# Gated heads in pairs with token-major values, and three orders outside the heads

## The chip, the cores and the metric

The kernel runs on one core of one Trainium2 chip. The metric is the time of one execution in device microseconds. Five engines work side by side from queues of their own: TensorE (PE) multiplies, VectorE (DVE) and ScalarE (ACT) work on elements and read and write TensorE's accumulators (PSUM), GpSimd (POOL) makes masks and issues transfers, SyncE (SP) issues the loads of the weights. They wait for one another by counting semaphores: `wait_ge(S[name], n)` holds the engine's queue until the counter has reached n.

## What is computed

Two transformer blocks over 512 tokens of 1024 channels, batch 1, one layer each, all in float32. What matters for the change is the mixing part of the first block and the start of attention in the second:

```python
# first block: 8 heads, each with a gated linear-attention branch (a) and a stick-breaking branch (b)
h = rms_norm(x, g); p = h @ w_in          # q_a k_a (64 wide) v_a o_a (128), i f, q_b k_b v_b (128), g_a g_b (128)
qk_a = silu(causal_conv([q_a, k_a], conv_w))
h_a  = head_rms_norm(mlstm(q_a, k_a, v_a, i, f)) # decay-masked scores times v_a, over a denominator
y_a  = sigmoid(o_a) * h_a
z    = rms(q_b) . rms(k_b) / sqrt(128)           # strictly causal
A    = sigmoid(z) * prod_{s<j<t} (1 - sigmoid(z_tj))
y_b  = A @ v_b
y    = sigmoid(g_a) * y_a + sigmoid(g_b) * y_b
x    = x + y @ w_out;  x = x + relu(rms_norm(x) @ w_up)**2 @ w_down
# second block: latent attention (8 heads), and sparse attention (8 heads), which sees the 128 best keys of an index
score = sum_h relu(q_idx_h . k_idx) * w_h        # 8 index heads
sel   = top_k(score, 128)                        # found in 16 rounds of 8
```

## The kernel before

**Projections.** All weights lie in one array `wall` of groups, 1024 x 512 each. SP loads a group in two halves into `w_raw`; ACT rounds a half to `w_hi` (`split_hi`, L257) and DVE makes the rest `w_lo` (`split_lo`, L264). `project` (L271) makes one tile, 128 x 512 results, by 24 matmuls: 8 row blocks times (hi x hi, hi x lo, lo x hi). Its first row block waits for the first half of the group's `w_lo`, its fifth for the second half. Tiles alternate between two PSUM banks `proj[:, 0]` and `proj[:, 1]`: tile n waits (`tile_free`) until tile n - 2 is evacuated, and `tile_made` counts finished tiles. `w_hi`/`w_lo` have two slots; a group's split waits until the group two before it has had its last tile.

**The heads of the first block.** A loop over eight heads on each engine; the order is written out by hand. Per head there are two groups and eight tiles, all feature-major (weight stationary, activation moving): 0 q_b, 1 k_b, 2 q_a with k_a, 3 v_b, 4 v_a, 5 o_a, 6 g_a, 7 g_b. PE's order (`head`, L1395) is: tiles 0, 1, 2; sums of squares of q_b and k_b into `pa` (L1424, L1425); tile 3; stick scores z into `pa` (L1430); tiles 4, 5; the turns of `v_bT` and `v_aT` to token-major in `pa` (L1439, eight transposes by matmul with the identity); gated scores into `pm` (L1446); tile 6; turns of the stick weights `beta` (L1456); weighted sums with `v_a` (L1462); tile 7; turns of `y_tok` (L1468); the weighted sum with `v_b` (L1411). The tiles between steps give ACT, DVE and POOL time for what the next step reads.

**What ACT does in a head.** It copies tiles out of `proj`, gives the roots (Ln, Exp), the Sigmoids of z (`beta`, `keep`) and of the convolution (`silu`), the Exp of `decay` (L581), copies of the turned values and sticks (L583 to L588), the row variances (L592). Gates o and g_a are first copied (L579, L586) and made Sigmoids in place later (L600, L601); g_b is a Sigmoid straight from `proj` (L603). Sigmoid and Exp lie in different tables, so there are table loads.

**What DVE and POOL do in a head.** DVE: `sq_lo`, norms of q_b and k_b, four taps of the convolution, `decay` arguments, silu, four scans (`kept`) and the product `beta`, then `split_lo`, then `decay` times scores (L1000); POOL masks its diagonal blocks (L449) before PE's weighted sums. `y_tok` (L1015) follows the variances; then the gated sums and y_hi, y_lo. `head_done` is counted at the end; the next head's squares wait for it.

**The start.** x comes in four tiles; each is scaled by DVE and turned by PE (`norm_pe`, L336); ACT and DVE make `h_hi` and `h_lo` (L319, L329); then come the gate tile (L1380), whose rows ACT and DVE work on, and the first head's tiles. Tile 2 waits for ACT's copy of tile 0, which stands behind the gate rows on ACT.

**The second block.** For each of four token blocks, `latents(t)` makes four tiles with few row blocks, which `latent_evac` (L681, copies at L689) takes out of `proj`. `idx_pair(p)` makes index scores of two heads in `pa` and `pm`; ACT's `idx_rel` (L701) takes them out as relus, 1280 columns each. Pair p waits for `2 * p` relus. On ACT, after the relus of pair 0, `latent_evac(2)` follows, and after those of pair 1, `latent_evac(3)`. In attention, B = 0 to 3 are pairs of latent heads and B = 4 to 7 pairs of sparse heads. DVE takes row maxima (L1250), divides (L1261), and in each B below 4 runs four rounds `top(B, rnd)` (L1267, L1271), each of which finds the next eight of each query's best keys. After 16 rounds the mask `idx` is made, which B = 4 needs.

Of the kernel before, what the change touches and what calls it, by code (L numbers as in the profile page):

```python
# [13 lines left out]
P = 128  # L14
# [8 lines left out]
DQK_A = 64  # L23
HD_B = 128
# [17 lines left out]
TRI_COLS = 1280  # L42

# [34 lines left out]
def program(nc, x_in, wall, gains, head_par, sb_gains, b_if, *rest):  # L78
    *block2_in, out = rest
    with ExitStack() as ctx:  # L80
# [41 lines left out]
        def at(name, offset, shape, dt=F32):  # L122
# [13 lines left out]
        names = "q_b k_b sq_q sq_k conv silu k_a v_bT v_aT v_b gate_o gate_a gate_b".split()  # L136
        (q_b, k_b, sq_q, sq_k, conv, silu, k_a, v_bT, v_aT, v_b, gate_o, gate_a, gate_b) = [
            at(n, (61 + 2 * i) * K, [P, SEQ]) for i, n in enumerate(names)]
        v_a = at("v_a", 87 * K, [P, TB, P + 1])
        y_tok, scl = sq_k, silu  # L140
# [272 lines left out]
        def _(pool):  # L413
# [11 lines left out]
            gp.memset(v_a[:, :, P:P + 1], 1.0).then_inc(S["consts"], 1)  # L425
# [73 lines left out]
        def _(act):  # L499
# [39 lines left out]
            with a.Fori(0, HEADS) as h:  # L539
                n = T_HEADS + 8 * h  # L540
                ga = G_HEADS + 2 * h

                a.preload_act_table_set("natural_log_exp_and_others")
                split_hi(ga + 1, 0, 0)

                for j, (raw, sq) in enumerate(((q_b, sq_q), (k_b, sq_k))):
                    a.wait_ge(S["tile_made"], n + j + 1)
                    a.wait_ge(S["head_done"], h + 1)
                    a.activation(raw[:, :], proj[:, j], ACT.Copy)
                    a.activation(sq_hi[:, j], proj[:, j], ACT.Square)  # L550
                    a.activation(sq[:, :], proj[:, j], ACT.Square).then_inc(S["tile_free"], 1)
                split_hi(ga + 1, 0, 1)

                a.wait_ge(S["tile_made"], n + 3)
# [9 lines left out]
                a.wait_ge(S["tile_made"], n + 4)  # L564
                a.activation(v_bT[:, :], proj[:, 1], ACT.Copy).then_inc(S["tile_free"], 1)
                split_hi(ga + 2, 1, 0)
# [5 lines left out]
                a.wait_ge(S["tile_made"], n + 5)  # L572
                a.activation(v_aT[:, :], proj[:, 0], ACT.Copy).then_inc(S["tile_free"], 1)

                a.activation(silu[:, :], conv[:, :], ACT.Sigmoid).then_inc(S["silu_sig"], 1)
                a.preload_act_table_set("natural_log_exp_and_others")
                split_hi(ga + 2, 1, 1)
                a.wait_ge(S["tile_made"], n + 6)
                a.activation(gate_o[:, :], proj[:, 1], ACT.Copy).then_inc(S["tile_free"], 1)  # L579
                a.wait_ge(S["arg_a"], 4 * h + 4)  # L580
                a.activation(decay[:, :], decay[:, :], ACT.Exp).then_inc(S["decay_exp"], 1)  # L581
                a.wait_ge(S["v_turned"], h + 1)
                a.activation(v_b[:, :], pa[:, 0:512], ACT.Copy).then_inc(S["v_sb"], 1)  # L583
                a.activation(v_a[:, :, 0:P], pa[:, 512:1024].rearrange("p (t n) -> p t n", t=TB), ACT.Copy).then_inc(S["v_sb"], 1)
                a.wait_ge(S["tile_made"], n + 7)
                a.activation(gate_a[:, :], proj[:, 0], ACT.Copy).then_inc(S["tile_free"], 1)  # L586
                a.wait_ge(S["a_turned_b"], h + 1)
                a.activation(aT[:, :], pa[:, 0:TRI_COLS], ACT.Copy).then_inc(S["a_b"], 1)  # L588

                a.wait_ge(S["num_made"], h + 1)  # L590
# [8 lines left out]
                a.wait_ge(S["tile_free"], n + 7)  # L599
                a.activation(gate_o[:, :], gate_o[:, :], ACT.Sigmoid).then_inc(S["gate_sig"], 1)  # L600
                a.activation(gate_a[:, :], gate_a[:, :], ACT.Sigmoid, bias=par[:, 5:6]).then_inc(S["gate_sig"], 1)  # L601
                a.wait_ge(S["tile_made"], n + 8)
                a.activation(gate_b[:, :], proj[:, 1], ACT.Sigmoid, bias=par[:, 6:7]).then_inc(S["tile_free"], 1)  # L603
# [134 lines left out]
            idx_rel(0)  # L738
            idx_rel(1)
            latent_root(1)  # L740
            for t in (2, 3):
                latent_evac(t)
                if t == 2:
                    evac(N_Q[1], q_b2[:, 1])
                latent_squares(t)
                idx_rel(2 * t - 2)
                idx_rel(2 * t - 1)
                latent_root(t)
# [152 lines left out]
        def _(dve):  # L901
# [4 lines left out]
            v.memset(tick[:, 2:3], 0.0).then_inc(S["pad_zero"], 1)  # L906
            def square_sum(t):
# [42 lines left out]
            with v.Fori(0, HEADS) as h:  # L950
                ga = G_HEADS + 2 * h

                v.wait_ge(S["head_done"], h + 1)
# [4 lines left out]
                split_lo(ga + 1, 0, 0)  # L958
                for j, sq in enumerate((sq_q, sq_k)):
                    v.wait_ge(S["tile_free"], T_HEADS + 8 * h + j + 1)  # L960
                    v.tensor_tensor(sq_lo[:, j], sq[:, :], sq_hi[:, j], ALU.subtract).then_inc(S["sq_lo"], 1)
                split_lo(ga + 1, 0, 1)
# [310 lines left out]
            for B in range(4):  # L1273
# [13 lines left out]
                for rnd in range(4):  # L1287
                    top(B, rnd)
# [83 lines left out]
        def _(pe):  # L1372
# [22 lines left out]
            def head(h, first=False):  # L1395
# [21 lines left out]
                if first:  # L1417
                    gate_rows()
# [55 lines left out]
            with t_.Fori(1, HEADS) as h:  # L1474
                head(h)
# [307 lines left out]
```

## Time and profile before

| | us |
|---|---|
| median of 3 runs | 1264.02 (1262.86 to 1264.53) |
| profiled execution, its own time | 1262.79 |
| its span, first to last instruction | 1260.5 |
| PE busy | 1240.2 (98%) |
| DVE busy | 694.1 (55%) |
| ACT busy | 606.6 (48%) |
| POOL busy | 47.8 (4%) |

The span is what the profile's times count in; the execution has 2.3 us around it. Busy PE includes modelled ends of matmuls, so a short wait between two of them can hide in it.

### The profile page before, as it was taken

The page shows a single profiled execution, that of the slowest core. Times are in us where ns is not written, and L with a number is a line of the kernel's source. Part 1 is how long each engine was busy: PE and PEld are TensorE (multiplying, and loading weights), DVE is VectorE, ACT ScalarE, POOL GpSimd, SP SyncE. Part 2 cuts the span into 40 slices and gives each one's busy share as a digit, 9 for nine tenths or more (in the row PEclk, how much of TensorE's full clock was granted, in tenths as well). Part 3 has the DMA queues.
Part 4 walks back from the last instruction along what each step waited for, and adds up shares of the span by engine and source line. Part 5 has one row for each costly group of instructions (what it writes and reads, how often), then busy time and mean ns, then how long its engine had stood idle before and what let it go on. Part 6 is the DMA issues. An engine that isn't in the chain of part 4 may idle for free.

```text
span 1260.5 us, 15952 instructions
## 1 busy us (share of the span) xinstructions
PE 1240.2 (98%) x5912; PEld 1008.2 (80%) x5912; DVE 694.1 (55%) x1179; ACT 606.6 (48%) x894; POOL 47.8 (4%) x146
## 2 busy tenths in 40 slices
PE   6999999999999999999999999999999999999998
PEld 5788888888888888888888888888867777677787
DVE  6646455554645555552443433445468989666671
ACT  6745565564556563441321421335456655566820
POOL 1000000000000020000000000000000000000000
PEclk9999999999999999999999999999999999999999
DMA  6323222132322234223231322333213233535621
GB/s 219 110 75 100 75 67 87 64 100 75 100 75 67 85 125 168 68 88 113 68 132 67 100 100 100 101 108 150 76 67 110 104 119 129 201 126 166 251 67 67
DMA packets 26398, 134.48 MB, mean 107 GB/s; under 512 B 3224, under 2 KB 4312, under 8 KB 13552
## 3 DMA queue, kind: packets, MB, share of 16 engines
q1 hardware_dynamic: 16992, 107.49, 25.3%
q0 software_dynamic: 4752, 16.92, 3.9%
q10 hardware_dynamic: 4608, 9.44, 2.0%
q8 instruction: 32, 0.52, 0.2%
q14 instruction: 14, 0.11, 0.0%
HBM read 122.28 MB, written 11.55 MB: 106 GB/s over the span
## 4 chain that ended last, share of the span: by engine, by line
PE 84%; DVE 10%; ACT 3%; issue 2%; DMA 1%; ACTq 0%; DVEq 0%; SPq 0%
PE proj L294 74%; DVE idx L1271 2%; DVE w_lo L267 2%; DVE top L1267 2%; PE pm L1462 1%; PE pa L1411 1%; PE pa L1430 1%; DVE p_sb L1250 1%; PE pm L1446 1%; PE pa L1648 1%; ACT w_hi L261 1%; PE pa L1456 1%; ACT p_sb L792 1%; DVE p_sb L1261 1%; DVE idx L1164 1%
## 5 line engine op out<-in xcount | busy, mean ns | idle before, releaser
L294 PE MATMUL proj<-h_hi,w_hi 128*128 128x512 f32 (+1 forms) x976 | 385.7, 395 | 2.0 <-DVE w_lo L267 1.0
L294 PE MATMUL proj<-h_hi,w_lo 128*128 128x512 f32 (+1 forms) x976 | 377.1, 386 | 0.0
L294 PE MATMUL proj<-h_lo,w_hi 128*128 128x512 f32 (+1 forms) x976 | 376.7, 386 | 0.0
L267 DVE TENSOR_TENSOR w_lo<-w_raw,w_hi 128x2048 fp32r<-128x2048 f32 x100 | 227.9, 2290 | 89.8 <-ACT w_hi L261 88.9
L261 ACT ACTIVATE w_hi<-w_raw 128x2048 fp32r<-128x2048 f32 x100 | 189.8, 1912 | 127.0 <-PE proj L294 121.3
L294 PEld LDWEIGHTS proj<-h_hi,w_hi 128*128 128x128 f32 x976 | 183.4, 188 | 46.0 <-issue 9.9
L294 PEld LDWEIGHTS proj<-h_lo,w_hi 128*128 128x128 f32 x976 | 183.5, 188 | 38.3 <-issue 2.9
L294 PEld LDWEIGHTS proj<-h_hi,w_lo 128*128 128x128 f32 x976 | 183.3, 188 | 37.5
L294 PE MATMUL proj<-w_hi,act_hi 128*128 128x512 f32 x256 | 99.8, 390 | 0.0
L294 PE MATMUL proj<-w_lo,act_hi 128*128 128x512 f32 x256 | 99.6, 389 | 0.0
L294 PE MATMUL proj<-w_hi,act_lo 128*128 128x512 f32 x256 | 99.6, 389 | 0.0
L1097 DVE TENSOR_TENSOR x_res<-x_res,proj 128x512 f32<-128x512 f32 x32 | 21.9, 686 | 92.2 <-PE proj L294 92.2
L633 ACT ACTIVATE relu<-proj 128x512 f32<-128x512 f32 x32 | 19.2, 599 | 106.5 <-PE proj L294 106.5
L1083 DVE TENSOR_TENSOR relu_sq<-relu 128x512 f32<-128x512 f32 x32 | 22.2, 694 | 73.4 <-ACT relu L633 73.4
L294 PE MATMUL proj<-w_hi,h_hi 128*128 128x512 f32 (+1 forms) x160 | 62.2, 389 | 0.0
L294 PE MATMUL proj<-w_lo,h_hi 128*128 128x512 f32 (+1 forms) x160 | 61.9, 387 | 0.0
L294 PE MATMUL proj<-w_hi,h_lo 128*128 128x512 f32 (+1 forms) x160 | 61.7, 386 | 0.0
L294 PEld LDWEIGHTS proj<-w_hi,act_lo 128*128 128x128 f32 x256 | 48.1, 188 | 10.0
L294 PEld LDWEIGHTS proj<-w_lo,act_hi 128*128 128x128 f32 x256 | 48.1, 188 | 10.0
L294 PEld LDWEIGHTS proj<-w_hi,act_hi 128*128 128x128 f32 x256 | 48.1, 188 | 9.8
L792 ACT ACTIVATE p_sb<-p_sb,mx 128x128 f32<-128x128 f32 (+1 forms) x64 | 35.1, 550 | 31.8 <-DVE mx L1253 31.8
L294 PEld LDWEIGHTS proj<-w_hi,h_hi 128*128 128x128 f32 x160 | 30.0, 188 | 7.4 <-issue 1.5
(394 smaller groups left out, 1650.2 us busy)
## 6 DMA issues: line engine op xcount, KB each, us to landing
w_raw<-in_wall SPq DMA_DIRECT2D x100, 1024.0 KB, 5.1
gates<-gate_st ACTq DMA_DIRECT2D x24, 256.0 KB, 2.1
m_all<-gates POOLq DMA_DIRECT2D x2, 1280.0 KB, 7.5
x_res<-in_x ACTq DMA_DIRECT2D x4, 512.0 KB, 5.2
bc<-gate_rows POOLq DMA_DIRECT2D x8, 256.0 KB, 3.5
x_res<-in_x POOLq DMA_DIRECT2D x4, 512.0 KB, 4.8
x<-x_res POOLq DMA_DIRECT2D x1, 2048.0 KB, 7.4
g_all<-gates POOLq DMA_DIRECT2D x1, 2048.0 KB, 11.2
```

The source lines that it names most:

```text
L261: nc.scalar.activation(w_hi[:, slot, 4 * half:4 * half + 4, :], w_raw[:, half], ACT.Copy)\
L267: nc.vector.tensor_tensor(w_lo[:, slot, 4 * half:4 * half + 4, :], w_raw[:, half], w_hi[:, slot, 4 * half:4 * half + 4, :], ALU.subtract)\
L294: mm = nc.tensor.matmul(proj[:, bank, 0:cols] if tokens else proj[:, bank, toks], lhsT, rhs, start=(k == 0 and q == 0), stop=(k == kts - 1 ...
L633: a.activation(relu[:, i % 2], proj[:, i % 2], ACT.Relu).then_inc(S["tile_free"], 1)
L792: a.activation(x, x, ACT.Exp, bias=mx[:, u, i:i + 1], accum_out=row_sum[:, u, i:i + 1])\
L1083: v.tensor_tensor(relu_sq[:, i % 2], relu[:, i % 2], relu[:, i % 2], ALU.mult).then_inc(S["a_sq"], 1)
L1097: v.tensor_tensor(xx, xx, proj[:, t % 2], ALU.add).then_inc(S["tile_free"], 1)
L1164: v.scalar_tensor_tensor(idx[:, c], rel[h % 2][:, c], w_idx[:, i, h:h + 1], idx[:, c] if h else causal[:, 384 - P * i:512], ALU.mult, ALU. ...
L1250: v.tensor_tensor_reduce(p_sb[u][:, c], X[:, c], mask(i), scale(i), -3.0e38, ALU.add, ALU.max, mx[:, u, i:i + 1]).then_inc(S[f"smax{u}"], 1)
L1261: v.tensor_scalar(x, x, row_sum[:, u, i:i + 1], None, ALU.mult).then_inc(S[f"p_norm{u}"], 1)
L1267: v.max(top8[:, i - 1, :], idx[:, LOW[i]:LOW[i] + P * (i + 1)]).then_inc(S["top_max"], 1)
L1271: v.match_replace(x, top8[:, i - 1, :], x, TAKEN).then_inc(S["top_out"], 1)
```

## The change

- **Pairs.** The heads run as four pairs, three in a loop and the last written out (`more=False`). A pair has four groups and sixteen tiles, numbered from 0: 0 q_b, 1 k_b, 2 q_a with k_a, 3 o_a (head one); 4 to 7 values; 8 g_a, 9 g_b (head one); 10 q_b, 11 k_b, 12 q_a with k_a, 13 o_a, 14 g_a, 15 g_b (head two). A pair's first two tiles are made inside the pair before (16 and 17, counted from its start); those of the first pair ahead of the loop.
- **Token-major values.** Tiles 4 to 7 are one token block each: activation stationary, weight moving, with v_b of both heads and v_a of both heads as 512 columns. ACT copies them straight to `v_b` and `v_a`. The turns of values, `v_bT` and `v_aT` are gone.
- **Gates.** o and g_a are made Sigmoids straight from `proj`; the copies are gone.
- **PE's order in a pair.** Head one: tile 2; squares; 3; z; 4, 5; gated scores; 6, 7; turns of beta; weighted sums; 8; turns of y; weighted sum with v_b. Head two: 9, 10, 11, 12; squares; 13; z; 14, 15; gated scores; 16; turns of beta; weighted sums; 17; turns of y; weighted sum with v_b. In the last pair 16 and 17 are left out.
- **pv_read.** The squares of a head wait for DVE's read of the last v_b sum, not for the whole head's end. `y_tok` has room of its own.
- **Outside the heads.** PE turns the identity 36 times before x is there (`WARM`). ACT's `latent_evac(2)` stands between `idx_rel(0)` and `idx_rel(1)`, `latent_evac(3)` between `idx_rel(2)` and `idx_rel(3)`. The first of the 16 rounds runs before B = 0; each of B = 0 to 2 has four rounds and B = 3 has three.

The core of the diff (the bodies of DVE's and ACT's steps, which only moved into functions, are left out):

```diff
+PAIRS = HEADS // 2
+QKA, O_A, VALUES, G_A, G_B, NEXT = (2, 12), (3, 13), 4, (8, 14), (9, 15), 16
+WARM = 36
@@ ACT
-            with a.Fori(0, HEADS) as h:
...
+            def qk_tile(n, heads, j):
+                raw, sq = ((q_b, sq_q), (k_b, sq_k))[j]
+                a.wait_ge(S["tile_made"], n + 1)
+                if heads is not None:
+                    a.wait_ge(S["z_made"], heads)
...
+            def gate_tile(n, dst, bias=0.0):
+                a.wait_ge(S["tile_made"], n + 1)
+                a.activation(dst[:, :], proj[:, 0 if dst is gate_a else 1], ACT.Sigmoid, bias=bias).then_inc(S["tile_free"], 1)
...
+            def value_tile(n, t):
+                a.wait_ge(S["tile_made"], n + VALUES + t + 1)
+                a.activation(v_b[:, :, t], proj[:, t % 2, 0:2 * P].rearrange("p (u d) -> p u d", u=2), ACT.Copy)
+                a.activation(v_a[:, :, t, 0:P], proj[:, t % 2, 2 * P:4 * P].rearrange("p (u d) -> p u d", u=2), ACT.Copy)\
+                    .then_inc(S["tile_free"], 1)
...
+                conv_tile(h, n + QKA[0])
+                gate_tile(n + O_A[0], gate_o)
+                split_hi(g + 2, 1, 0)
+                sticks(h)
+                value_tile(n, 0)
+                a.preload_act_table_set("natural_log_exp_and_others")
+                split_hi(g + 2, 1, 1)
+                value_tile(n, 1)
+                decays(h)
+                value_tile(n, 2)
+                value_tile(n, 3)
+                stick_turns(h)
+                variance(h)
+                split_hi(g + 3, 0, 0)
+                gate_tile(n + G_A[0], gate_a, par[:, 5:6])
+                split_hi(g + 3, 0, 1)
+                gate_tile(n + G_B[0], gate_b, par[:, 6:7])
+                h = 2 * p + 1
+                a.preload_act_table_set("natural_log_exp_and_others")
+                for j in range(2):
+                    qk_tile(n + 10 + j, 2 * p + 1, j)
+                conv_tile(h, n + QKA[1])
+                gate_tile(n + O_A[1], gate_o)
+                split_hi(g + 4, 1, 0)
+                sticks(h)
+                split_hi(g + 4, 1, 1)
+                a.wait_ge(S["par_head"], 3 * h + 3)
+                gate_tile(n + G_A[1], gate_a, par[:, 5:6])
+                gate_tile(n + G_B[1], gate_b, par[:, 6:7])
+                a.preload_act_table_set("natural_log_exp_and_others")
+                decays(h)
+                if more:
+                    split_hi(g + 5, 0, 0)
+                    qk_tile(n + NEXT, 2 * p + 2, 0)
+                stick_turns(h)
+                variance(h)
+                if more:
+                    qk_tile(n + NEXT + 1, 2 * p + 2, 1)
+                    split_hi(g + 5, 0, 1)
@@ ACT, second block
             idx_rel(0)
+            latent_evac(2)
             idx_rel(1)
             latent_root(1)
-            for t in (2, 3):
...
+            evac(N_Q[1], q_b2[:, 1])
+            latent_squares(2)
+            idx_rel(2)
+            latent_evac(3)
+            idx_rel(3)
+            latent_root(2)
@@ DVE (head two of a pair; head one has the same steps)
+                head_start(h)
+                for j in range(2):
+                    square_low(n + 10 + j, j)
+                qk_norms(h)
+                conv_taps(h, n + QKA[1])
+                split_lo(g + 4, 1, 0)
+                decay_args(h)
+                gated_keys(h)
+                sticks(h)
+                split_lo(g + 4, 1, 1)
+                gated_scores(h)
+                if more:
+                    split_lo(g + 5, 0, 0)
+                    v.wait_ge(S["a_done"], h + 1)
+                    square_low(n + NEXT, 0)
+                token_norm(h)
+                gated_y(h, n + O_A[1], n + G_A[1])
+                if more:
+                    square_low(n + NEXT + 1, 1)
+                head_end(h, n + G_B[1])
+                if more:
+                    split_lo(g + 5, 0, 1)
@@ DVE, attention
+            top(0, 0)
             for B in range(4):
...
-                for rnd in range(4):
-                    top(B, rnd)
+                for rnd in range(4 * B + 1, min(4 * B + 5, 16)):
+                    top(rnd // 4, rnd % 4)
@@ PE
+            for i in range(WARM):
+                t_.transpose(pm[:, 1024 + P * (i % 4):1024 + P * (i % 4 + 1)], ident[:, :], ident[:, :])
...
+            def pair(p, more=True):
+                n_v = T_HEADS + 16 * p + VALUES
+                for u in range(2):
+                    h = 2 * p + u
+                    if u:
+                        for j in (9, 10, 11):
+                            head_tile(p, j)
+                    head_tile(p, QKA[u])
+                    square_sums(h)
+                    head_tile(p, O_A[u])
+                    stick_scores(h)
+                    head_tile(p, G_A[1] if u else VALUES)
+                    head_tile(p, G_B[1] if u else VALUES + 1)
+                    gated_scores(h)
+                    if u == 0:
+                        head_tile(p, VALUES + 2)
+                        head_tile(p, VALUES + 3)
+                    elif more:
+                        head_tile(p, NEXT)
+                    stick_turns(h)
+                    gated_sums(h, u, n_v)
+                    if u == 0:
+                        head_tile(p, G_A[0])
+                    elif more:
+                        head_tile(p, NEXT + 1)
+                    head_turns(h, u)
```

## Rows read from the trace of the kernel before

**Rows 1.** The page: busy time of the engines, and the granted clock in 40 slices.

```profile
PE 1240.2 (98%) x5912; PEld 1008.2 (80%) x5912; DVE 694.1 (55%) x1179; ACT 606.6 (48%) x894; POOL 47.8 (4%) x146
...
PEclk9999999999999999999999999999999999999999
```

**Rows 2.** The waits of PE: us in total, times, longest us.

```profile
PE proj L336 <- DVE xs L324: 8.1, 1, 8.1
```

**Rows 3.** Timeline of PE at the start: start, us, line, operands, idle before.

```profile
8.51 0.84 PE L336 MATMUL pa<-ident,xs 128*128 128x128 f32 x3
...
13.73 0.49 PE L336 MATMUL pm<-ident,xs 128*128 128x128 f32 x3
...
35.35 0.50 PE L294 MATMUL proj<-h_hi,w_hi 128*128 128x512 f32 x1 [0.96 <-ACT sq_q L551]
```

**Rows 4.** Timeline of DVE at the start.

```profile
14.35 1.41 DVE L329 SCALAR_TENSOR_TENSOR h_lo<-proj,gain,h_hi 128x512 fp32r<-128x512 f32 x2 [0.69 <-ACT h_hi L319]
```

**Rows 5.** Timeline of PE in the last head.

```profile
446.96 0.60 PE L1439 MATMUL pa<-ident,v_bT 128*128 128x128 f32 x4
...
447.92 0.69 PE L1446 MATMUL pm<-silu,k_a 64*128 64x512 f32 x1
...
449.41 0.50 PE L294 MATMUL proj<-h_hi,w_hi 128*128 128x512 f32 x1
...
455.01 1.25 PE L1456 MATMUL pa<-ident,beta 128*128 128x128 f32 x10
456.10 2.40 PE L1462 MATMUL pm<-v_a,decay 128*128 128x129 f32 x20
458.25 0.48 PE L294 MATMUL proj<-h_hi,w_hi 128*128 128x512 f32 x1
```

**Rows 6.** Timeline of ACT in the last head.

```profile
447.65 1.26 ACT L581 ACTIVATE decay<-decay 128x1280 f32<-128x1280 f32 x1
...
464.01 0.69 ACT L603 ACTIVATE gate_b<-proj,par 128x512 f32<-128x512 f32 x1 [0.51 <-PE proj L294]
464.71 1.28 ACT L604 ACT_TABLE_LOAD   x1
```

**Rows 7.** Timeline of DVE and POOL in the last head.

```profile
448.98 2.28 DVE L267 TENSOR_TENSOR w_lo<-w_raw,w_hi 128x2048 fp32r<-128x2048 f32 x1
451.18 1.49 DVE L1000 SCALAR_TENSOR_TENSOR decay<-pm,decay 128x1280 f32<-128x1280 f32 x1
...
460.97 0.69 DVE L1015 TENSOR_TENSOR sq_k<-pm,tok 128x512 f32<-128x512 f32 x1 [0.51 <-ACT tok L597]
...
452.74 1.03 POOL L449 TENSOR_SCALAR_AFFINE_SELECT decay<-decay 128x128 f32<-128x128 f32 x4 [10.44 <-DVE decay L1000]
```

**Rows 8.** Timeline of PE, then of ACT, at the latent tiles.

```profile
930.25 0.50 PE L294 MATMUL proj<-w_hi,ckv_hi 128*128 128x512 f32 x1 [1.08 <-ACT q_a L689]
...
943.38 0.51 PE L294 MATMUL proj<-w_hi,ckv_hi 128*128 128x512 f32 x1 [1.08 <-ACT q_a L689]
...
944.98 0.37 PE L1547 MATMUL pa<-t_c 32*128 32x128 f32 x1
...
941.18 1.23 ACT L701 ACTIVATE rel<-pm 128x1280 f32<-128x1280 f32 x1
...
945.09 0.60 ACT L689 ACTIVATE v_a<-proj 128x512 f32<-128x512 f32 x1
```

**Rows 9.** Timeline of DVE, then of PE, around the rounds.

```profile
970.55 0.35 DVE L1250 CUSTOM_DVE_ANT_0 p_sb<-pm,causal,qk_ss 128x128 f32<-128x128 f32 x1 [2.72 <-issue]
...
1073.85 0.42 DVE L1267 MAX8 top<-idx 128x8 f32<-128x256 f32 x1
...
1077.07 0.23 DVE L1291 COPY idx<-causal 128x128 f32<-128x128 f32 x1
...
1087.46 1.31 PE L1639 MATMUL pm<-ident,p_sb 128*128 128x128 f32 x10 [1.81 <-DVE p_sb L1261]
1088.86 1.31 PE L1639 MATMUL pa<-ident,p_sb 128*128 128x128 f32 x10
```

More of the change, by code:

```diff
@@ L135, in program @@
         bc = at("bc", 57 * K, [P, SEQ])
[L136 to L140, printed above, removed]
+        q_b, k_b, sq_q, sq_k, conv, silu, k_a = [
+            at(n, (61 + 2 * i) * K, [P, SEQ]) for i, n in enumerate("q_b k_b sq_q sq_k conv silu k_a".split())]
+        v_b = at("v_b", 75 * K, [P, 2, TB, P])
+        gate_o, gate_a, gate_b = [at(n, (79 + 2 * i) * K, [P, SEQ]) for i, n in enumerate(("gate_o", "gate_a", "gate_b"))]
+        v_a = at("v_a", 85 * K, [P, 2, TB, P + 1])
+        y_tok, scl = at("y_tok", 59 * K, [P, SEQ]), silu
         qk_pad = at("qk_pad", 47 * K, [P, 3 + SEQ])
@@ L604, in _ @@
+            with a.Fori(0, PAIRS - 1) as p:
+                pair(p)
+            pair(PAIRS - 1, more=False)
             a.preload_act_table_set("natural_log_exp_and_others")
@@ L1470, in head, with pair @@
                 t_.wait_ge(S["a_b"], h + 1)
[L1471 to L1475 removed]
+                for i in range(TB):
+                    mm = t_.matmul(pa[:, P * i:SEQ], v_b[:, u, i], aT[:, TRI[i]:TRI[i] + SEQ - P * i],
+                                   start=(i == 0), stop=(i == TB - 1))
+                mm.then_inc(S["pv_b_made"], 1)
+            def pair(p, more=True):
+                n_v = T_HEADS + 16 * p + VALUES
[10 more added lines that the diff above has]
+                    head_tile(p, G_B[1] if u else VALUES + 1)
+                    gated_scores(h)
+                    if u == 0:
[10 more added lines that the diff above has]
+                    head_turns(h, u)
+            head_tile(0, 0, first=True)
+            head_tile(0, 1)
+            gate_rows()
+            with t_.Fori(0, PAIRS - 1) as p:
+                pair(p)
+            pair(PAIRS - 1, more=False)
             t_.wait_ge(S["head_done"], HEADS)
@@ L1708, in lay_out, with wide, narrow @@
     wall[G_GATES, :, :, 32:32 + HEADS] = f_a
-    for h in range(HEADS):
-        wide, narrow = slice(P * h, P * (h + 1)), slice(DQK_A * h, DQK_A * (h + 1))
-        wall[G_HEADS + 2 * h] = np.concatenate(
-            [q_b[:, :, wide], k_b[:, :, wide], q_a[:, :, narrow], k_a[:, :, narrow], v_b[:, :, wide]], axis=2)
-        wall[G_HEADS + 2 * h + 1] = np.concatenate([w[:, :, wide] for w in (v_a, o_a, g_a, g_b)], axis=2)
+    def wide(w, h):
+        return w[:, :, P * h:P * (h + 1)]
+    def narrow(w, h):
+        return w[:, :, DQK_A * h:DQK_A * (h + 1)]
+    for p in range(PAIRS):
+        h, i = 2 * p, 2 * p + 1
+        for k, columns in enumerate((
+                (wide(q_b, h), wide(k_b, h), narrow(q_a, h), narrow(k_a, h), wide(o_a, h)),
+                (wide(v_b, h), wide(v_b, i), wide(v_a, h), wide(v_a, i)),
+                (wide(g_a, h), wide(g_b, h), wide(q_b, i), wide(k_b, i)),
+                (narrow(q_a, i), narrow(k_a, i), wide(o_a, i), wide(g_a, i), wide(g_b, i)))):
+            wall[G_HEADS + 4 * p + k] = np.concatenate(columns, axis=2)
     for j in range(2):
```

180 lines of the change are left out of this document (84 added, 96 removed).

## Prediction

> **What bounds the kernel now.** I read the page's busy line first. PE is busy for 98% of the span [rows 1], so a microsecond counts only where PE loses work or where PE waits. DVE at 55% and ACT at 48% matter where PE waits for them. Next I read the waits of PE: its largest entry is the 8.1 us before the first turn [rows 2]. Then I followed the timeline through four places: the start [rows 3, 4], one head [rows 5 to 7], the latent tiles [rows 8] and the sparse half of attention [rows 9]. Matmul ends are modelled there, so I go by starts: 24 matmuls of a tile and the step to the next work take 5.60 us (449.41 to 455.01), 0.23 each. A head is a string of such tiles with PE never waiting. It holds eight tiles before and eight after, so order alone wins nothing there; only PE work that goes, and waits that come, count.
>
> **Part 1, the start: -0.7 us.** The turns of x run at half pace first: three from first start to last end take 0.84 us at 8.51 and 0.49 us at 13.73 [rows 3]. The 36 added turns of the identity (0.21 us each at the low pace, 7.5 us; fewer when the pace has risen) about fill the 8.1 us of [rows 2]. An overrun of a microsecond harms nothing: the x turns behind them, at the full pace, would still catch up with DVE, which scales x tile by tile. They end earlier, about with the last scaled tile. But the end of this stage is not PE's. DVE waits 0.69 us for the first h_hi, until 14.35 [rows 4]; only this can go, for DVE has other work before it and works without a break behind it. The chain runs on through the gate rows to ACT's evacuation, for which PE waits at 35.35 [rows 3]: that start moves to 34.7. Bounds: 1.2 earlier (if the first projection tile, not the gate rows, sets the rest), and 2.5 later if the pace falls back in the pause that the earlier turns leave ahead of the gate matmuls. I take -0.7, because the wait of DVE is a row.
>
> **Part 2a, the heads' work: -7.2 us.** The eight turns of v_bT and v_aT go. PE starts them at 446.96 and the scores behind them at 447.92 [rows 5]: 0.96 us per head, 7.7 for eight. No row shows a projection tile followed at once by the 64-row scores. The step may cost nothing new or up to 0.1 more (8 x 0.1 = 0.8); I take 7.2, a little over half of this off; bounds 6.9 and 7.7. Values are made token by token instead (activation stationary, weight moving). These matmuls are as many and as wide, and cost the same: nothing. ACT loses two gate copies per head and gains none. DVE's work is the same and POOL's and SP's too.
>
> **Part 2b, the pairs' new order: 0 in the first seven heads.** The tightest places, counted in the last head's frame: the scores now end at 448.45 (0.96 before 449.41). In an odd head the next q tile follows at once and asks for the second w_lo half at its fourth row block, 12 x 0.23 later, 451.2. DVE ended that half at 451.26 before [rows 7], but the Sigmoid of conv no longer stands behind the v_aT copy on ACT, which brings DVE's chain about 1.5 us forward: not late. In an even head the sums follow the turns of beta (1.09) and ask for the last value tile's copies, two of 256 columns; ACT is free for them, and I find 0.1 us to spare: nothing, at most 0.3 x 4. The new wait of head_end on the tile of g_b leaves three tiles before pa is wanted again.
>
> **Part 2c, the last head: +7.1 us.** Here no tile is left between the scores and the turns of beta, nor between the sums and the turns of y; before, tiles 6 and 7 stood there. So two waits come into the open:
> - The sums wait for the masked decay. The tile of g_b ends at 446.96 and its Sigmoid starts 0.2 later: 447.2. Behind it on ACT: Sigmoid 0.69, table load 1.28, exponential 1.26 [rows 6], to 450.4. Then DVE's product, whose mask starts 1.56 after it (451.18 to 452.74), and the mask 1.03 [rows 7]: 453.0. PE is through with the turns of beta at 448.45 + 1.09 = 449.55 [rows 5] and waits 3.6 us (start 453.15).
> - The turns of y wait for y_tok. Sums start at 456.10 [rows 5], y_tok ends at 461.66 [rows 7]: 5.56 later. PE's sums take 2.15 of this (456.10 to 458.25). The wait is 5.56 - 2.15 + 0.1 = 3.5 us.
> Together 7.1. Bounds: 5.5 (table load hidden and the y chain a little shorter) and 8.5 (one weight split of 1.9 more ahead of the exponential). In the run of heads the change is thus worth -7.2 + 7.1, about nothing: what the turns give back, the empty last head takes.
>
> **Part 3, the latent tiles: -0.35 us.** PE waits at 930.25 and 943.38 for the copy of q_a, 1.08 each [rows 8], because two relus of 1.23 stand ahead of it. With one relu ahead, the copy starts when its tile is ready: the first wait goes whole, -1.1. The second goes too (943.38 becomes 942.3), but what is late next? The index scores at 944.98 need the fourth relu, now behind the four copies. The v_a copy started at 945.09; 1.1 earlier is 944.0, half a microsecond on ACT, then a relu of 1.24 ends at 945.7: 0.75 later than 944.98. The two together: -1.1 + 0.75. Bounds -1.1 and +1.5.
>
> **Part 4, the first round of the top values: -2.2 us.** At 1087.46 PE waits 1.81 by the view, 1.97 by starts (a modelled matmul end lies 0.16 behind the next start), and 0.25 more before the second batch (1.40 from 1087.46 to 1088.86, where ten turns take 1.09). DVE is late: its last round ran from 1073.85 to 1077.07, 3.2 us [rows 9]. One round now stands ahead of the first latent head, where DVE sat idle for 2.72 before 970.55 and a little more before the weight split ahead of that: 3.2 us about fit. The wait needs 2.2 and gets 3.2. Bounds -2.3 and -1.0 (if the early round delays the maxima).
>
> **Sum**, against the profiled execution's own 1262.8 us: -0.7 - 7.2 + 7.1 - 0.35 - 2.2 = -3.35, hence 1259.4. The median of the runs lies 1.2 above that execution, so I forecast 1264.0 - 3.4 = 1260.6.
>
> **A rule that speaks against it.** In this trace the granted clock never falls in any slice [rows 1], through waits of up to 2.2 us from start to start; the longest behind the start is the one before 1087.46 [rows 9]. The last head will have 3.6 and 3.5 us of wait, with 2.15 of work between. The Trainium skill ("TensorE: Matmul & The Clock Gate", section "HAM oscillation") says that a long enough idle stretch between bursts of matmuls throws the array back to its lower clock, so that the next burst starts slow. By the trace's longest wait alone the sum stays; by that page the second rival below happens. No row here decides it.
>
> **The rivals.**
> - *Shorter waits in the last head* (4.5 instead of 7.1): the chains pass through small ACT and DVE steps that may start earlier. 1258.0. For it: 1.28 of the first chain is a table load, which ACT may take while it waits for the tile. Against it: that load needs the table of exponentials, and the Sigmoid ahead needs the other.
> - *The clock falls in the last head.* After 8.1 idle us the low pace lasted about 5.1 us of work (from 8.1 to about 13.2) [rows 2, 3]. Half pace over 5.1 us costs 2.5; if the sums between the waits run slowly too, 2.1 more. Together 2.5 to 4.7 on the forecast: 1263.1 to 1265.3, I say 1264.0, no change.
> - *Slower: the splits come late at the next q tile.* ACT now has a table load and a Sigmoid of o_a ahead of the split and of beta (1.28 + 0.63, where one copy of 0.6 stood). If DVE's chain of scans, product and split comes x us later than I reckon, the q tile waits x - 1.5 in each of three odd heads, and the last head x - 0.8. From x = 2.2 this eats the 3.4 us, and at x = 3 it gives 4.5 + 2.2 - 3.4 = +3.3: 1267.3. For it: w_lo ended within 0.1 us of that point before. Against: the silu wait that goes is longer than the load that comes.
> - *The first round moves the wait, not the work*: if the maxima of the first latent head slip by what DVE gains later, part 4 gives 0: 1262.8.
>
> **How the numbers follow.** Forecast 0.50 (own range 1258.6 to 1262.4), shorter waits 0.14, clock falls 0.17, slower 0.11, moved wait 0.08. A measurement of this kernel can tell about 0.2% (2.5 us) from no change: faster means below 1261.5, slower above 1266.5. Faster: 0.40 of the forecast, 0.13 of the shorter waits and 0.02 of the others, 0.55. Slower: 0.08 of the slower case and 0.01 of the clock, 0.09. Same: 0.36. For 8 in 10 the range is 1256.5 to 1265.5.
>
> **What would show it.** Right: no row of v_bT or v_aT; each head 0.9 us shorter than before; no PE wait over 0.5 us in the first seven heads; in the last, about 3.6 before the sums and 3.5 before the turns of y; the index scores of the third pair waiting about 1.9; no wait before the turns of p_sb in the first sparse head; granted clock 1.00 from the start on. Wrong: waits at the q tile in the middle of odd heads; ten turns taking 2.1 us behind the last head's waits; a pause over 0.5 us before the sums in even heads.

## The result, and the profile after

The changed kernel is slower: 1268.26 us median (1265.66 to 1270.32, 14 runs) where the kernel before has 1264.49 (1262.5 to 1267.4, 14 runs) on the same chip, ratio 1.0027, 95% interval 1.0019 to 1.0035. The forecast was 1260.6, with 1256.5 to 1265.5 as its range. The profiled execution after took 1269.27, its span is 1267.3.

The page after, busy time of the engines and the granted clock in 40 slices, answers to [rows 1]:

```profile
PE 1246.1 (98%) x5884; PEld 1011.0 (80%) x5884; DVE 694.4 (55%) x1180; ACT 580.3 (46%) x871; POOL 71.1 (6%) x146
...
PEclk9899999999999989999999999999999999999999
```

PE has 28 instructions fewer (36 more turns of the identity, 64 fewer of the values) and is busy for 5.9 us more. Less work that takes longer is slower work, and two slices of PEclk stand at 8. The same in stretches, PE alone (us, busy time and count, granted clock, DMA share, GB/s):

```profile
13.00:20.00 7.00, 4.32 (x13) 0.76 0.65 240
...
36.00:44.00 8.00, 7.24 (x19) 0.57 0.60 179
44.00:460.00 416.00, 415.24 (x1935) 1.00 0.25 81
460.00:475.00 15.00, 9.22 (x36) 0.77 0.35 127
...
940.00:954.00 14.00, 12.15 (x68) 1.00 0.00 1
954.00:962.00 8.00, 8.00 (x30) 0.79 0.00 0
```

Behind the first 6 us the granted clock is 1.00 but for five stretches, in which it is 0.5 (1.2 of 2.4 GHz): from 15.7 (3.4 us), 36.1 (6.8), 462.8, 469.6 and 954.3 (3.4 each). I call such a drop a fall of the clock. In the profile before it is 1.00 at all of these places. Each stretch begins within 0.7 us of the end of a wait, just before it or just behind, but for the last, 1.8 behind one. The waits of PE after (us in total, times, longest):

```profile
PE pm L1560 <- POOL decay L453: 3.3, 1, 3.3
PE pm L1567 <- DVE y_tok L1077: 3.2, 1, 3.2
PE proj L1501 <- DVE h_lo L333: 2.7, 1, 2.7
PE proj L298 <- ACT sq_q L551: 2.3, 1, 2.3
PE pa L1679 <- ACT rel L751: 1.8, 1, 1.8
```

They are the two of the last head, the one before the gate matmuls, the one before tile 2, and the one before the indexer's fifth tile. PE's timeline at four of them:

```profile
12.56 0.49 PE L340 MATMUL pm<-ident,xs 128*128 128x128 f32 x3
15.73 0.76 PE L1501 MATMUL proj<-h_hi,wg_hi 128*128 128x512 f32 x1 [2.68 <-DVE h_lo L333]
...
36.76 0.79 PE L298 MATMUL proj<-h_hi,w_hi 128*128 128x512 f32 x1 [2.29 <-ACT sq_q L551]
...
457.92 1.31 PE L1551 MATMUL pa<-ident,beta 128*128 128x128 f32 x10
462.56 4.14 PE L1560 MATMUL pm<-v_a,decay 128*128 128x129 f32 x20 [3.33 <-POOL decay L453]
469.92 1.12 PE L1567 MATMUL pm<-ident,y_tok 128*128 128x128 f32 x4 [3.21 <-DVE y_tok L1077]
470.83 3.43 PE L1571 MATMUL pa<-aT,v_b 128*128 128x512 f32 x8
...
474.01 0.47 PE L298 MATMUL proj<-w_hi,y_hi 128*128 128x512 f32 x1
```

The twenty sums took 2.40 before [rows 5] and take 4.14 now. A matmul of 512 columns that starts every 0.23 us at the full clock starts every 0.43 inside these stretches.

The stages by starts of PE, for before, after, and the experiment with filler in four of the five waits (e8, below). The boundaries after are these rows (the square sums of heads 0, 2 and 6, the first scores of the sparse half and its first output tile; the first output tile of the gated half is the last row above):

```profile
45.22 0.39 PE L1525 MATMUL pa<-sq_hi,ones_r 128*128 128x512 f32 x1
...
154.04 0.39 PE L1525 MATMUL pa<-sq_hi,ones_r 128*128 128x512 f32 x1
...
371.71 0.39 PE L1525 MATMUL pa<-sq_hi,ones_r 128*128 128x512 f32 x1
...
977.27 0.60 PE L1732 MATMUL pm<-kT,qT 96*128 96x128 f32 x3
...
1176.29 0.50 PE L298 MATMUL proj<-og_hi,w_hi 128*128 128x512 f32 x1
```

| Stage | before, us | after | forecast | with filler |
|---|---|---|---|---|
| to the first square sums | 40.92 | +4.30 | -0.7 | +0.64 |
| six heads | 331.38 | -4.89 | -5.4 | -4.90 |
| last two heads | 94.02 | +8.28 | +5.3 | +5.14 |
| to the sparse scores | 501.86 | +1.40 | -0.35 | -0.24 |
| to the sparse output | 201.33 | -2.31 | -2.2 | -2.31 |
| the rest | 91.03 | +0.01 | 0 | -0.02 |
| span | 1260.54 | +6.79 | -3.35 | -1.69 |

Six of the eight heads, the sparse half and the rest went as forecast. The three stages that hold the five slow stretches went wrong by 5.0, 3.0 and 1.75 us. With filler the same three are shorter by 3.66, 3.14 and 1.64; in the first of them 0.65 is no clock, for there the gate matmuls start at 15.08 instead of 15.73, with weights that came earlier.

### The profile page after: what moved, and what is told of

The parts are those of the page before. It is cut to its first block, busy times and chain, and to the rows that moved or that the text cites. A ratio compares the mean times of both kernels' runs of the same rounds, so it can differ in the third digit from the quotient of the medians.

```text
span 1267.3 us, 15778 instructions
## 1 busy us (share of the span) xinstructions
PE 1246.1 (98%) x5884; PEld 1011.0 (80%) x5884; DVE 694.4 (55%) x1180; ACT 580.3 (46%) x871; POOL 71.1 (6%) x146
## 4 chain that ended last, share of the span: by engine, by line
PE 92%; DVE 5%; ACT 1%; issue 1%; DMA 1%; POOL 0%; ACTq 0%; SPq 0%; DVEq 0%
PE proj L298 79%; PE pm L1560 2%; PE pa L1571 1%; PE pa L1532 1%; PE pa L1780 1%; DVE w_lo L271 1%; PE pm L1542 1%; PE pa L1679 1%; PE pa L1760 1%; DVE idx L1389 1%; PE pa L1771 1%; PE pa L1551 1%; PE proj L1501 1%; DVE p_sb L1368 1%; PE pm L1771 1%
## 5 line engine op out<-in xcount | busy, mean ns | idle before, releaser
L298 PE MATMUL proj<-h_hi,w_hi 128*128 128x512 f32 (+1 forms) x848 | 334.6, 395 | 2.3 <-ACT sq_q L551 2.3
L298 PE MATMUL proj<-h_hi,w_lo 128*128 128x512 f32 (+1 forms) x848 | 328.0, 387 | 0.0
L298 PE MATMUL proj<-h_lo,w_hi 128*128 128x512 f32 (+1 forms) x848 | 327.9, 387 | 0.0
L298 PEld LDWEIGHTS proj<-h_hi,w_hi 128*128 128x128 f32 x848 | 160.1, 189 | 39.0 <-issue 7.3
L298 PE MATMUL proj<-w_hi,h_hi 128*128 128x512 f32 (+1 forms) x288 | 114.6, 398 | 0.0
L298 PE MATMUL proj<-w_hi,h_lo 128*128 128x512 f32 (+1 forms) x288 | 112.1, 389 | 0.0
L298 PE MATMUL proj<-w_lo,h_hi 128*128 128x512 f32 (+1 forms) x288 | 112.1, 389 | 0.0
L298 PEld LDWEIGHTS proj<-w_hi,h_hi 128*128 128x128 f32 x288 | 54.4, 189 | 15.1 <-issue 4.3
L298 PEld LDWEIGHTS proj<-w_hi,h_lo 128*128 128x128 f32 x288 | 54.4, 189 | 11.5 <-issue 1.0
L298 PEld LDWEIGHTS proj<-w_lo,h_hi 128*128 128x128 f32 x288 | 54.4, 189 | 10.7
```

The source lines that it names most:

```text
L298: mm = nc.tensor.matmul(proj[:, bank, 0:cols] if tokens else proj[:, bank, toks], lhsT, rhs, start=(k == 0 and q == 0), stop=(k == kts - 1 ...
```

## The experiments

Theory: the change makes five waits of PE longer or new; behind them the granted clock falls, and the work there runs at half pace. Rivals: the waits themselves cost more than reckoned, or one part alone is to blame. All runs were timed in five rounds against the kernel before on the same chip. Where a difference is said to be by the ratio, it is the ratio's distance from 1, of 1264 us.

**One part undone, or filler in one place.** e1_no_warm takes the early turns out, e2_latent3 moves one copy back, e3_fill gives PE 30 turns of the identity that nothing reads in each of the last head's two waits.

```diff
 e1_no_warm
-WARM = 36
+WARM = 0
 e2_latent3
             idx_rel(2)
-            latent_evac(3)
             idx_rel(3)
             latent_root(2)
+            latent_evac(3)
 e3_fill (the same lines once more behind gated_sums)
                     stick_turns(h)
+                    if u and not more:
+                        fill(p, 30)
                     gated_sums(h, u, n_v)
```

> The changed kernel without the 36 turns of the identity ahead of x (WARM = 0), all else kept. Theory (the clock): the turns let the x turns end 1.3 us earlier, the pause before the gate matmuls grows from 1.7 to 2.8 us, the clock falls in it, the gate rows come 1.4 us late and the clock falls again in the longer wait behind them; by the profile the start costs 4.3 us. Without the turns PE starts tile 2 at about 35.4 again, the clock stays at 1.00 from 13 us on, and the kernel takes 4 us less than the changed one: about 1264.3. Rival (the turns help by the 0.7 us I forecast, and the clock falls there whatever precedes): 1269, and low clock at 16 and at 36 us remains.

> The changed kernel with latent_evac(3) put back behind idx_rel(3) on ACT; latent_evac(2) stays between the first two relus. Theory (the clock): the wait of 2.0 us before the third pair of index scores goes and with it the fall of the clock at 954 us, which costs about 2 us in the profile; the wait of 1.24 us before the third tile of that block comes back. Together 2.8 us less than the changed kernel, about 1265.5. Rival (the new order only trades one wait for another): 0.75 us less, about 1267.5.

> The changed kernel with 30 turns of the identity into an idle accumulator bank in each of the two waits of the last head (before the weighted sums and before the turns of y), 3.3 us each: no wait gets shorter and no work goes. Theory (the clock): the two falls at 462.8 and 469.6 us go, and sums, turns and the v_b sum run at full pace: 3.3 us less than the changed kernel, about 1265.0. Rival (the waits themselves are the cost): within 0.5 us of the changed kernel, 1268.3.

Measured: e1_no_warm 1266.11 (11 runs), ratio 1.0017 (1.0008 to 1.0026); e2_latent3 1265.51 (11), 1.0015 (1.0006 to 1.0024); e3_fill 1265.88 (11), 1.0014 (1.0004 to 1.0023); before 1263.8 (27). They were expected at 1264.3, 1265.5 and 1265.0. By the ratio each gives back 1.3 to 1.6 us of the changed kernel's 3.4, about what the two intervals together leave open (1.5); what is clear is that each is still slower than before, so undoing one part alone does not give the whole back. In e1_no_warm the fall at the gate matmuls is gone, but those before tile 2 (at 35.9) and in the last head are there. In e3_fill the last head keeps its clock, and the indexer's wait still loses it (PE's columns as above):

```profile
455.00:470.00 15.00, 14.94 (x103) 1.00 0.48 175
944.00:952.00 8.00, 7.70 (x25) 0.57 0.00 0
```

**Filler in four of the five places.** e8_fill_all is e3_fill with 20 more turns ahead of tile 2 and 16 ahead of the indexer's fifth tile; the wait before the gate matmuls has none.

```diff
+            for i in range(20):
+                t_.transpose(pa[:, P * (i % 4):P * (i % 4 + 1)], ident[:, :], ident[:, :])
             with t_.Fori(0, PAIRS - 1) as p:
...
             latents(3)
+            for i in range(16):
+                t_.transpose(pa[:, 1408:1536], ident[:, :], ident[:, :])
             idx_pair(2)
```

> The kernel after with turns of the identity that nothing reads in TensorE's waits: 30 in each of the two of the last head, 20 ahead of tile 2, 16 ahead of the second pair of the indexer's tiles. No wait is removed and no real work changed. Theory (the loss against the forecast is the clock): the granted clock stays full in all but the pause before the gate matmuls, and the time goes to 1261.5, below before's 1263.8, though the kernel only got more to do. Rival (the loss is in the waits themselves or in work that grew): the time stays at 1265 or above, as with the filler in the last head alone (1265.9).

Measured: 1260.89 us (1259.92 to 1263.59, 9 runs), ratio 0.9972 (0.9960 to 0.9984); before 1264.33 (26). A kernel that does strictly more than the changed one is 0.55% faster than it. PE's timeline in its last head and at the indexer:

```profile
454.26 1.31 PE L1551 MATMUL pa<-ident,beta 128*128 128x128 f32 x10
455.41 3.44 PE L1578 MATMUL proj<-ident 128*128 128x128 f32 x30
458.91 2.50 PE L1560 MATMUL pm<-v_a,decay 128*128 128x129 f32 x20
461.25 3.44 PE L1578 MATMUL proj<-ident 128*128 128x128 f32 x30
464.63 0.66 PE L1567 MATMUL pm<-ident,y_tok 128*128 128x128 f32 x4
465.12 2.32 PE L1571 MATMUL pa<-aT,v_b 128*128 128x512 f32 x8
467.20 0.47 PE L298 MATMUL proj<-w_hi,y_hi 128*128 128x512 f32 x1
...
943.67 1.91 PE L1721 MATMUL pa<-ident 128*128 128x128 f32 x16
945.65 0.37 PE L1690 MATMUL pa<-t_c 32*128 32x128 f32 x1
```

The sums take 2.50 instead of 4.14; from the turns of beta to the first output tile it is 12.94 us instead of 16.09. The real work waits as long as before; only the array isn't idle. The one fall left lies at the gate matmuls, the one wait without filler (from 14.7 us, 3.4 us). This is the last column of the table: within 1.7 us of the forecast, 1.3 of them in the first stage.

**Each part alone, on the kernel before.** e5_before_warm adds the 36 turns only, e6_before_round the first round only, e10_latents_only the latents' order only, e9_heads_only the pairs only (both orders and the early turns taken out of the kernel after). e11_heads_fill is e9 with e3's filler.

```diff
 e5_before_warm
+            for i in range(36):
+                t_.transpose(pm[:, 1024 + P * (i % 4):1024 + P * (i % 4 + 1)], ident[:, :], ident[:, :])
             norm_pe(0)
 e6_before_round
+            top(0, 0)
             for B in range(4):
...
-                for rnd in range(4):
-                    top(B, rnd)
+                for rnd in range(4 * B + 1, min(4 * B + 5, 16)):
+                    top(rnd // 4, rnd % 4)
 e10_latents_only
             idx_rel(0)
+            latent_evac(2)
             idx_rel(1)
             latent_root(1)
-            for t in (2, 3):
-                latent_evac(t)
...
+            evac(N_Q[1], q_b2[:, 1])
+            latent_squares(2)
+            idx_rel(2)
+            latent_evac(3)
+            idx_rel(3)
+            latent_root(2)
```

> The kernel before with only the 36 turns of the identity added ahead of the turns of x. Theory (the clock is lost in waits that the change itself made longer): the turns of x end about 1.3 us earlier, h_lo's last step does not follow because the low weights landed no earlier, so the pause of TensorE before the gate matmuls grows from 1.97 us to some 2.8 us; in part of the executions the granted clock falls to half in it, and the eight gate matmuls and what follows run at 0.43 us each. That takes what the early turns give and more: 1 to 2 us above before, about 1265.0 where before has 1263.8. Rival (the early turns are worth their 0.7 us, and the loss lies in the last head and the latents alone): 0.7 us below before, 1263.1.

> The kernel before with only the order of the first round changed (the top of batch 0's first round issued ahead of the rest). Theory: this part acts alone and by the size forecast, the stretch from the first key turn to the first output group gets 2.2 us shorter and the granted clock stays full: 1261.6 where before has 1263.8. Rival (the wait moves to the next round, or the clock falls where the early work has left a gap): no change, 1263.8.

> The kernel before with only the heads in pairs and token-major values: no early turns of the identity, the old order of the latent tiles and of the first round. Theory: the heads are worth -6.5 us and the last head's two longer waits +7.1 us, which is +0.6 us at the full clock; behind these waits the granted clock falls, and the sums and turns at half pace cost 2 to 3 us more: 1266.5 to 1267.5 where before has 1264.3. Rival (the last head costs its waits alone): 1264.9.

> The kernel before with only the order of the latent tiles among the indexer's relus changed. Theory: two waits of 0.6 us go and one of about 2.2 us comes ahead of the indexer's fifth tile; at the full clock that is -0.35 us, and in the executions in which the clock falls behind that wait, 3.4 us run at half pace, 1.7 us: 1264 to 1265.5 where before has 1264.3. Rival (the clock does not fall in this place without the other parts): 1263.9.

> The heads alone, as in the run beside it, with 30 turns of the identity that nothing reads in each of the last head's two waits. Theory: the waits stay as long, the granted clock stays full, and the 2 to 3 us of matmuls at half pace go: 1264.5 to 1265 where before has 1264.3. Rival (the clock falls for another reason, or the filler holds up the sums): no lower than the heads alone, 1266.5 or more.

| Run | us (runs) | expected | ratio, 95% interval | median clock | at the same mean clock |
|---|---|---|---|---|---|
| early turns alone | 1265.09 (12) | 1265.0 | 1.0006 (0.9994 to 1.0017) | 0.997 | -0.5 to -0.9 |
| first round alone | 1260.36 (12) | 1261.6 | 0.9973 (0.9962 to 0.9984) | 1.000 | -2.6 to -2.8 |
| latents' order alone | 1267.27 (12) | 1264 to 1265.5 | 1.0020 (1.0009 to 1.0030) | 0.996 | 0 to -0.5 |
| heads alone | 1267.94 (12) | 1266.5 to 1267.5 | 1.0024 (1.0012 to 1.0035) | 0.995 | -0.4 |
| heads with filler | 1263.69 (12) | 1264.5 to 1265 | 0.9997 (0.9987 to 1.0007) | 0.999 | 0 to -0.4 |
| before, beside the first two and the last three | 1264.33 (26), 1264.35 (29) | | | 0.999 | |

The last column is worth a look of its own. Each execution has a mean granted clock, and this one compares a run's executions with those of before at the same mean clock (mean times in us, wherever both have some; the cells have 1 to 10 executions each, and for the heads alone only 0.997 is shared). There the four parts come out near what was forecast for them at the full clock: -0.7, -2.2, -0.35 and -0.1. The rest of what the medians show goes with the lower clocks at which the executions lie. The mean counts a fall by its length and not by the work in it, so this is a check and no exact price.

The ratios of the four parts add up to +0.23% where the whole change is +0.27%. The filler in two waits takes 4.3 us off the heads alone. Their last head without and with it, the same 14 us of PE (two kernels, one fence each):

```profile
460.00:474.00 14.00, 9.02 (x30) 0.51 0.33 125
```

```profile
460.00:474.00 14.00, 14.00 (x87) 1.00 0.53 155
```

The profile of the heads alone also shows the two falls of the start, from 16.6 and 37.1 us (3.4 each), behind waits of 2.35 and 2.50 from start to start, though this kernel has no early turns. So those two places can lose their clock without them.

The latents' order alone was a miss: 1264 to 1265.5 expected, 1267.3 found. Two waits of 1.08 before, one of 1.81 now, as forecast, and the clock falls behind it for 6.8 us. Its timeline of PE, then its stretches, then a second fall, of 3.4 us, behind the wait ahead of the first sparse head, which the kernel before has too:

```profile
944.76 0.37 PE L1550 MATMUL pa<-t_c 32*128 32x128 f32 x1 [1.81 <-ACT rel L701]
...
946.56 0.84 PE L1550 MATMUL pa<-t_c 32*128 32x384 f32 x1
```

```profile
930.00:945.00 15.00, 13.15 (x66) 1.00 0.00 0
945.00:952.00 7.00, 7.00 (x23) 0.51 0.02 4
```

```profile
1090.53 1.31 PE L1642 MATMUL pm<-ident,p_sb 128*128 128x128 f32 x10 [1.83 <-DVE p_sb L1264]
1091.92 2.39 PE L1642 MATMUL pa<-ident,p_sb 128*128 128x128 f32 x10
```

Its twelve executions are a scale of their own: 1262.06 at a mean clock of 1.000, 1265.65 to 1265.91 at 0.997, 1267.12 to 1267.66 at 0.996, 1269.39 at 0.995. The profile, with both falls, is one of the seven at 0.996. So the miss has two terms: the fall at the indexer lasted 6.8 us where 3.4 had been reckoned, and the one at 1092 was not in the theory at all. The one that kept the clock, 1262.06, stands beside nine executions of before at 1.000, which took 1262.0 to 1262.9.

The early turns alone stay unclear in the timing. At the same mean clock they gain 0.5 to 0.9 us, but 5 of their 12 executions lie at 0.996, and 2 of 26 of before; that takes it back. Their trace shows what bounds the gain. First ACT, then PE:

```profile
11.90 1.06 ACT L520 ACTIVATE wg_hi<-wg_raw 128x1024 fp32r<-128x1024 f32 x1 [1.16 <-DMA wg_raw<-in_wall]
```

```profile
15.78 0.47 PE L1382 MATMUL proj<-h_hi,wg_hi 128*128 128x512 f32 x1 [2.92 <-DVE h_lo L329]
```

The gate matmuls wait for the gate weights' DMA. In 13 profiles the first step on these weights starts between 10.79 and 12.28 us, and the gate matmuls start 3.88 behind it in nine of them. The other four are all without the early turns (they are half of the eight such profiles): there the chain over the turns of x is the later one, by 0.1 to 0.9 us. So by the profiles the part can give that much in half of the executions, a little less than the comparison at the same clock says; which is nearer stays open.

The first round alone is worth more than its forecast: 3.4 by the ratio (4.0 between the medians) instead of 2.2, and 2.6 at the same clock. In its profile, as in the changed kernel's, the stage to the sparse output is 2.31 shorter. The wait that it removes is one behind which the kernel before loses its clock in some executions. The trace of the early turns alone, in which that wait of before still stands, shows it (PE):

```profile
1085.00:1089.40 4.40, 2.49 (x17) 1.00 1.00 310
1089.40:1092.80 3.40, 3.40 (x14) 0.50 0.88 306
```

**A better version.** e4_early takes the early turns out, moves the latents' copy back and puts real work in the last head's waits: seven of eight row blocks of the first output tile ahead of the sums, of the second ahead of the turns of y, of the third (in pa) behind the sum over v_b. e7_adds_first also lets VectorE's first three output adds go ahead of its weight splits.

```diff
 e4_early
                     stick_turns(h)
+                    if u and not more:
+                        t_.wait_ge(S["head_done"], HEADS)
+                        out_rows(0, range(7))
                     gated_sums(h, u, n_v)
+                    if u and not more:
+                        out_rows(1, range(7))
...
+            out_rows(2, range(7))
+            t_.wait_ge(S["head_done"], HEADS + 1)
+            for i in range(3):
+                made(out_rows(i, (7,)))
 e7_adds_first, VectorE's output groups
-                split_lo(g + 1, (g + 1) % 2, 0)
+                if g > G_OUT:
+                    split_lo(g + 1, (g + 1) % 2, 0)
...
+                    if t == 2 and g == G_OUT:
+                        for hf in (0, 1):
+                            split_lo(g + 1, (g + 1) % 2, hf)
```

> The changed kernel without the identity turns, with latent_evac(3) back, and with real work in the last head's waits: seven of eight row blocks of the first output tile before the weighted sums, seven of the second before the turns of y, seven of the third (in a free bank of pa) behind the v_b sum; the last row blocks follow when the last head is done. Theory: nothing of the 7.1 us of waits is left, the clock never falls, and what stays is the gain of the removed turns (6.6), of the first latent order (1.1) and of the first round (2.2): 9.9 us below the kernel before, about 1254.6. Rival (the order in pairs costs something of its own beside the waits that I name): 1258 or more.

> e4_early with VectorE's first three output adds ahead of the splits of the first output group, so that the fourth output tile finds its bank free. Theory: the wait of 2.7 us at 477 us and the fall of the clock behind it go, 2.7 us and 1 to 2 us of matmuls at half pace: 1252 to 1253 where e4_early had 1255.5 (before 1263.8). Rival (the splits are now late, and the output group behind waits for them for as long): 1255 to 1256, with a wait of 2 us or more for the splits in the next group.

Measured: e4_early 1255.53 us (5 runs; 1254.6 expected), ratio 0.9939 (0.9925 to 0.9952), with one wait that the moved work brought, 2.71 from start to start, and a fall of 3.4 us behind it:

```profile
PE proj L298 <- DVE x_res L1165: 2.3, 1, 2.3
```

e7_adds_first 1254.82 (6 runs; 1252 to 1253 expected), ratio 0.9929 (0.9909 to 0.9948), median clock 1.000: that wait is down to 0.3 and its fall is gone, but a wait of 1.92 (start to start) has come at 494.8, behind which the clock held:

```profile
494.84 1.09 PE L366 MATMUL pa<-ident,xs 128*128 128x128 f32 x8 [1.53 <-DVE xs L358]
```

PE waits there for DVE's scaled x, which stands behind the next group's splits; so the rival was partly right. It beats both kernels: 9.5 us below before between the medians, 9.0 by the ratio.

## Why the prediction was wrong

- **Part 1, -0.7 (found +4.3): failed twice.** The wait of 0.69 in [rows 4] was read as a constant; it belongs to an execution in which the weights landed early. And "2.5 later if the pace falls back in the pause" was named as a bound and left out of the sum. The pause grew to 2.95 us from start to start (12.78 to 15.73), the clock fell there and again before tile 2. At the same mean clock the part alone is worth 0.5 to 0.9, so its size was sound; the loss is the clock's, and the heads alone lose it in the same two places.
- **Part 2a, -7.2: right, 0.6 too large.** Two heads take 108.82 us (45.22 to 154.04) where they took 110.47: 0.82 per head, 6.6 for eight, just under the bound of 6.9.
- **Part 2b, 0: right.** No new wait in the first seven heads (the one before tile 2 belongs to the start); the rival of late splits did not happen.
- **Part 2c, +7.1: right at the full clock.** The waits are 3.60 and 3.49 from start to start (3.6 and 3.5 forecast). With filler the two last heads take +5.14; their two shares of the turns are -1.65, so the waits cost 6.8. The rival of shorter waits is refuted. What was not in the sum is 3.1 us of sums, turns and v_b sums at half pace.
- **Part 3, -0.35: right at the full clock (-0.24), wrong in sum (+1.4).** The late relu was found to 0.1 us, 1.8 where I said 1.9; I put a price of 0.75 on it and none on the clock.
- **Part 4, -2.2: right, -2.31** by starts. Alone it gave 3.4 by the ratio, more than was forecast, since a wait at which before itself loses its clock in some executions went with it.

The step that failed is the one sentence "granted clock 1.00 from the start on". It rested on [rows 1] and on waits up to 2.2 us through which the clock held [rows 9]. But that profile is one of the executions at 1.000; before's median is 0.999 and goes down to 0.996, and another trace shows the fall behind that very wait. The rival *the clock falls in the last head* had the mechanism, 0.17 of the chance, and 2.5 to 4.7 us for one place, where 3.1 came; two more places had it. The start and the indexer stood in the sum with no price on the clock. The rule of the Trainium skill ("TensorE: Matmul & The Clock Gate", section "HAM oscillation") agrees with the falls behind the waits of 3.60 and 3.49. I had weighed it against those two alone, and the clock fell behind 2.95, 2.50 and 2.21 as well, while it held through 2.75 and 3.19 in other executions; there the runs decide, and not that rule.

In this kernel the loss can be read off the mean clock. After: 1 - 0.992 of 1267 us is 10 us of full clock missing, some of it over idle time. Between the profiles after and e8 lie 8.5 us of span (6.79 + 1.69), 7.8 of them for the four falls that went and 0.65 for the earlier weights; 1268.26 - 1260.89 is 7.4 in the medians.

## What to carry to other kernels

A wait of TensorE costs its length and then the half pace behind it, here 1.5 to 1.6 us for each 3.4 us of low clock with nearly full work. At the latent tiles two short waits were cheaper than one longer wait in their place, though their sum was larger (1.0020 for the new order alone). Before adding up, list the waits that the change makes longer than any that held; where they can't go, give PE work that is due later (e7_adds_first, 9.5 us below before) or filler (e8_fill_all, 7.4 below the changed kernel). A row of one execution that hangs on a DMA's landing, or on a clock that happened to hold, is a sample: look at the spread of the runs' clocks first, and compare two kernels also at the same mean clock: it tells what a change gives from what the clock takes.

## What the runs showed that I had not expected

- Whether the clock falls is not settled by the wait's length alone. From start to start, it fell behind 1.72 (e11_heads_fill, tile 2), 1.86 (e1_no_warm, tile 2), 2.21 (indexer), 2.22 (first sparse head), 2.35, 2.50, 2.67, 2.71, 2.82, 2.95 and every wait of 3.49 or more, and held through 2.13 (e3_fill, tile 2), 2.20 (heads alone, first sparse head), 2.21 (e1_no_warm, indexer), 2.45 (e11_heads_fill, gate matmuls), 2.75 (e3_fill, gate matmuls) and 3.19 (e5_before_warm, gate matmuls). The same wait of 2.21 at the indexer fell in e3_fill and held in e1_no_warm. Ahead of the wait at tile 2, where the shortest ones fell, PE has only eight turns of 8 columns, but it has them in e3_fill too. What decides between them stays open.
- The low clock lasted 3.4, 6.8 or 13.7 us, never less. The longest, in the heads alone and in e1_no_warm, spans both waits of the last head.
- The first step on the gate weights, which waits for their load in every profile, started up to 1.5 us apart in executions of kernels whose loads are the same there.
